# A two-layer hybrid-attention encoder on one core: where the grid heads' bias, values and outputs are issued, and when their probabilities are transposed

## The reference, cut to what matters

```python
sc = jnp.einsum('bnmiphd,bnmjqhd->bnmhipjq', qg, kg, ...) * (d ** -0.5)
sc = sc + bias.transpose(1, 2, 0, 3, 4, 5, 6)...[None]     # rpb: a learnt bias by row and column distance
sc = jnp.where(mask[:, :, None][None], sc, NEG_INF)
p = jax.nn.softmax(...)
o = jnp.einsum('bnmhipjq,bnmjqhd->bnmiphd', p.astype(v.dtype), vg)
```

## Time and profile before

| | us |
|---|---|
| median of 3 runs | 3005.68 (3001.18 to 3006.33) |
| the profiled execution | 3012.73 |
| its span | 3010.9 |
| TensorE busy | 2890.4 (96%) |
| VectorE, ScalarE, GpSimd busy | 1720.6, 1056.8, 26.3 |
| mean granted TensorE clock | 0.976 of full |

### The profile page before, as it was taken

The page is one execution under the profiler, slowest core; times in us unless marked ns, Lnnn a source line. Parts: engine busy times, 40 slices in busy tenths (PEclk is TensorE's granted clock), DMA queues, the critical chain, the costliest instruction groups (busy, mean ns, idle before and its releaser), DMA issues.

```text
span 3010.9 us, 39890 instructions
## 1 busy us (share of the span) xinstructions
PE 2890.4 (96%) x14640; PEld 2469.6 (82%) x14640; DVE 1720.6 (57%) x2998; ACT 1056.8 (35%) x1976; POOL 26.3 (1%) x53
## 2 busy tenths in 40 slices
PE   7999889998999999999999998999899999999998
PEld 7998777887888888888798987788788888888887
DVE  5642666885454554555666346678755555555457
ACT  5332655784311111111244245567742111111113
POOL 0000000000000000000000000000000000000000
PEclk9999989999999999999999998999999999999999
DMA  5656765323011111111146577553131111111111
GB/s 190 188 173 173 170 143 126 90 62 119 29 56 42 45 53 42 56 42 63 44 174 198 168 189 155 133 123 85 43 112 43 56 42 42 56 42 56 42 60 68
DMA packets 211031, 285.31 MB, mean 95 GB/s; under 512 B 64208, under 2 KB 170320, under 8 KB 201168
## 3 DMA queue, kind: packets, MB, share of 16 engines
q1 hardware_dynamic: 207056, 266.76, 31.5%
q0 software_dynamic: 3840, 16.78, 1.5%
HBM read 210.60 MB, written 72.88 MB: 94 GB/s over the span
## 4 chain that ended last, share of the span: by engine, by line
PE 81%; DVE 5%; DMA 5%; issue 3%; SPq 3%; ACT 2%; DVEq 1%; ACTq 0%; POOLq 0%
PE ps L1384 23%; PE ps L1213 20%; PE ps L1399 17%; PE ps L1286 7%; PE ps L1300 5%; PE ps L1329 4%; DMA head<-feats 3%; PE ps L1339 1%; PE ps L1181 1%; PE ps L1250 1%; DMA values<-vst 1%; SPq L463 1%; DVE x L1134 1%; SPq L488 1%; PE ps L1322 1%
## 5 line engine op out<-in xcount | busy, mean ns | idle before, releaser
L1399 PE MATMUL ps<-w_dn,hid 128*128 128x512 f32 x3072 | 712.9, 391 | 1.4
L1384 PE MATMUL ps<-hT,w_up 128*128 128x512 f32 x3072 | 702.5, 390 | 3.3 <-DVE hT L871 3.3
L1399 PEld LDWEIGHTS ps<-w_dn,hid 128*128 128x128 f32 x3072 | 573.8, 188 | 131.7 <-DVE x L1134 14.1
L1384 PEld LDWEIGHTS ps<-hT,w_up 128*128 128x128 f32 x3072 | 576.4, 188 | 122.9 <-ACT rbuf L821 3.7
L1213 PE MATMUL ps<-ws,hT 128*128 128x384 f32 (+3 forms) x3072 | 609.6, 357 | 2.6 <-issue 1.6
L1213 PEld LDWEIGHTS ps<-ws,hT 128*128 128x128 f32 x3072 | 538.1, 191 | 48.8 <-issue 2.4
L1134 DVE TENSOR_TENSOR x<-ps,x 128x512 f32<-128x512 f32 x512 | 342.8, 689 | 223.5 <-PE ps L1399 223.2
L772 ACT ACTIVATE pT<-ps 128x512 fp32r<-128x512 f32 (+1 forms) x448 | 240.2, 581 | 185.6 <-PE ps L1300 183.9
L1121 DVE TENSOR_TENSOR vbuf<-rbuf 128x512 f32<-128x512 f32 x128 | 88.6, 692 | 371.0 <-ACT rbuf L821 371.0
L871 DVE TENSOR_TENSOR pT<-ps,pT 128x512 fp32r<-128x512 f32 (+1 forms) x448 | 281.5, 664 | 8.6 <-ACT pT L772 6.7
L779 ACT ACTIVATE prob<-ps,a_nm 128x1024 f32<-128x1024 f32 (+1 forms) x256 | 252.6, 987 | 65.6 <-DVE a_nm L1036 49.7
(11 more groups left out here) (82 smaller groups left out, 2063.7 us busy)
## 6 DMA issues: line engine op xcount, KB each, us to landing
raw<-in_wstream SPq DMA_DIRECT2D x76, 1024.0 KB, 4.9
head<-feats SPq DMA_DIRECT2D x192, 256.0 KB, 6.4
feats<-tst SPq DMA_DIRECT2D x128, 192.0 KB, 2.6
values<-vst POOLq DMA_DIRECT2D x32, 384.0 KB, 3.2
head<-values SPq DMA_DIRECT2D x24, 512.0 KB, 4.2
biasC<-in_bias_c SPq DMA_DIRECT2D x16, 768.0 KB, 9.6
raw<-in_wstream SPq DMA_DIRECT2D x12, 768.0 KB, 5.9
x_park<-x SPq DMA_DIRECT2D x16, 512.0 KB, 9.4
```

The source lines that it names most:

```text
L1384: last = pe.matmul(ps[:, k % 2, :], w_up[0 if first else 1][:, w1, kt, ft * P:(ft + 1) * P], hT[:, w2, kt, sh * 512:(sh + 1) * 512], start ...
L1399: last = pe.matmul(ps[:, 2 + m % 4, :], hid[slot][:, w1, ft, s * P:(s + 1) * P], w_dn[1 if last_group else 0][:, w2, ft, nh * 512:(nh + 1) ...
```

## The change

A grid head's two bias halves are issued directly behind its features. Its sixteen value transfers, the eight transfers of a finished grid head's output and the one that reads it back are issued by GpSimd's queue instead of SP's, with the same waits and a semaphore of their own for the values. GpSimd waits for the end of the projections and of all their stores first. The transposes of a C item come three steps behind its scores instead of two; those of A and B stay at two. The weighing of a C block follows its transposes and so moves by one step as well. Where the kinds change from C to A, one step then has the transposes of two items.

```diff
--- before.py
+++ after.py
@@ -88,7 +88,7 @@
 NB = NI // 4
 GRID_BEFORE = [sum(kind_ == "C" for kind_, _, _ in ITEMS[:n_]) for n_ in range(NI)]
 STEPS = NI + 12
-TURN_STEP = [n_ + 2 for n_ in range(NI)]
+TURN_STEP = [n_ + (3 if kind_ == "C" else 2) for n_, (kind_, _, _) in enumerate(ITEMS)]
 WEIGH_STEP = [TURN_STEP[4 * b_ + 3] + 1 for b_ in range(NB)]
 
 
@@ -315,7 +315,7 @@
         tab_in, kr_in = sem("tab_in"), sem("kr_in")
         head_in = [sem(f"head_in{k}") for k in range(2)]
         value_in = [sem(f"value_in{k}") for k in range(2)]
-        grid_parked, grid_back = sem("grid_parked"), sem("grid_back")
+        grid_v_in, grid_parked, grid_back = sem("grid_v_in"), sem("grid_parked"), sem("grid_back")
         biasc_in = [sem(f"biasc_in{k}") for k in range(2)]
         s_done, mx_ready, p_ready = sem("s_done"), sem("mx_ready"), sem("p_ready")
         t_done, t_hi, t_lo = sem("t_done"), sem("t_hi"), sem("t_lo")
@@ -415,31 +415,11 @@
 
                 kind, h = HEADS[n]
                 load_features(l, n)
-                if n >= 3 and HEADS[n - 3][0] == "C":
-                    read_grid(l, HEADS[n - 3][1] - HA - HB)
                 if kind == "C":
                     load_bias(l, 2 * (h - HA - HB))
-                load_values(l, n)
-                if n >= 2 and HEADS[n - 2][0] == "C":
-                    park_grid(l, n - 2)
-                if kind == "C":
                     load_bias(l, 2 * (h - HA - HB) + 1)
-
-            def park_grid(l, n):
-
-                k = HEADS[n][1] - HA - HB
-                sp.wait_ge(o_ready, l * NB + 2 * n + 2)
-                rows = grid_out[k].rearrange("(f r c) d -> f r c d", f=2, c=GRID_W)
-                for t in range(8):
-                    cb, hf = t // 2, t % 2
-                    sp.dma_start(rows[hf, :, 16 * cb:16 * cb + 16, :], oC[k % 2][:, t, :]).then_inc(grid_parked, 16)
-
-            def read_grid(l, k):
-
-                h = HA + HB + k
-                sp.wait_ge(grid_parked, (l * HC + k + 1) * 8 * 16)
-                sp.dma_start(O[:, :, h * HD:(h + 1) * HD], grid_out[k].rearrange("(t p) d -> p t d", p=P))\
-                  .then_inc(grid_back, 16)
+                else:
+                    load_values(l, n)
 
             def load_bias(l, nc_half):
                 if nc_half >= 2:
@@ -475,18 +455,9 @@
                 hb = words(head[k][:, :])
                 if n >= 2:
                     sp.wait_ge(pv_done, l * NB + 2 * (n - 1))
-                if kind != "C":
-                    sp.dma_start(hb[:, 4096:5120].rearrange("p (t d) -> p t d", d=P),
-                                 values[:, h * P:(h + 1) * P].rearrange("(t p) d -> p t d", p=P))\
-                      .then_inc(value_in[k], 16)
-                else:
-                    grid = values.rearrange("(r c) d -> r c d", c=GRID_W)
-                    for cb in range(4):
-                        for rr in range(4):
-                            dst = hb[32 * rr:32 * rr + 32, 3072 + 512 * cb:3072 + 512 * (cb + 1)]
-                            src = grid[rr:rr + 13:4, c_cols(cb):c_cols(cb) + CKC, h * P:(h + 1) * P]
-                            sp.dma_start(dst.rearrange("c (g d) -> c g d", d=P),
-                                         src.rearrange("g c d -> c g d")).then_inc(value_in[k], 16)
+                sp.dma_start(hb[:, 4096:5120].rearrange("p (t d) -> p t d", d=P),
+                             values[:, h * P:(h + 1) * P].rearrange("(t p) d -> p t d", p=P))\
+                  .then_inc(value_in[k], 16)
 
             def stores_done(l):
 
@@ -602,6 +573,38 @@
         def _(pool):
 
             pool.memset(eps[:, :], EPS).then_inc(eps_set, 1)
+
+            def load_grid_values(l, n):
+
+                h, k = HEADS[n][1], n % 2
+                if n >= 2:
+                    pool.wait_ge(pv_done, l * NB + 2 * (n - 1))
+                grid = values.rearrange("(r c) d -> r c d", c=GRID_W)
+                for cb in range(4):
+                    for rr in range(4):
+                        dst = words(head[k][32 * rr:32 * rr + 32, 3072 + 512 * cb:3072 + 512 * (cb + 1)])
+                        src = grid[rr:rr + 13:4, c_cols(cb):c_cols(cb) + CKC, h * P:(h + 1) * P]
+                        pool.dma_start(dst.rearrange("c (g d) -> c g d", d=P),
+                                       src.rearrange("g c d -> c g d")).then_inc(grid_v_in, 16)
+
+            def park_grid(l, n):
+
+                k = HEADS[n][1] - HA - HB
+                pool.wait_ge(o_ready, l * NB + 2 * n + 2)
+                rows = grid_out[k].rearrange("(f r c) d -> f r c d", f=2, c=GRID_W)
+                for t in range(8):
+                    cb, hf = t // 2, t % 2
+                    pool.dma_start(rows[hf, :, 16 * cb:16 * cb + 16, :], oC[k % 2][:, t, :])\
+                        .then_inc(grid_parked, 16)
+
+            def read_grid(l, n):
+
+                h = HEADS[n][1]
+                k = h - HA - HB
+                pool.wait_ge(grid_parked, (l * HC + k + 1) * 8 * 16)
+                pool.dma_start(O[:, :, h * HD:(h + 1) * HD], grid_out[k].rearrange("(t p) d -> p t d", p=P))\
+                    .then_inc(grid_back, 16)
+
             for l in range(DEPTH):
                 for vt, e in enumerate(VSTAGED):
                     k = vt % 2
@@ -610,6 +613,23 @@
                     h0, nh = {"uv": (0, HA), "bv": (HA, HB), "cv": (HA + HB, HC)}[e[1]]
                     pool.dma_start(values[e[2] * P:(e[2] + 1) * P, h0 * P:(h0 + nh) * P],
                                    words(vst[:, k, 0:nh, :].rearrange("p h d -> p (h d)"))).then_inc(vst_out[k], 16)
+                pool.wait_ge(acc_done, l * len(ACCS) + job_end("cv"))
+                hold(pool)
+                for k in range(NTS):
+                    pool.wait_ge(tst_out[k], (l + 1) * 16 * TST_N[k])
+                    hold(pool)
+                for k in range(2):
+                    pool.wait_ge(vst_out[k], (l + 1) * 16 * (len(VSTAGED) // 2))
+                    hold(pool)
+                grids = [n for n in range(NH) if HEADS[n][0] == "C"]
+                for n in grids:
+                    load_grid_values(l, n)
+                    if n > grids[0]:
+                        park_grid(l, n - 2)
+                        read_grid(l, n - 2)
+                park_grid(l, grids[-1])
+                read_grid(l, grids[-1])
+
 
         @block.scalar
         def _(act):
@@ -1309,8 +1329,11 @@
                     if part == 0:
                         pe.wait_ge(t_lo, l * NGR + ITEM_GROUPS[4 * b + 3][-1] + 1)
                         n, k = b // 2, b // 2 % 2
-                        done = sum(VALUE_DMAS[kd] for kd, _ in HEADS[k:n + 1:2])
-                        pe.wait_ge(value_in[k], (l * VALUE_N[k] + done) * 16)
+                        if kind == "C":
+                            pe.wait_ge(grid_v_in, (l * HC + h - HA - HB + 1) * 16 * 16)
+                        else:
+                            done = sum(kd != "C" for kd, _ in HEADS[k:n + 1:2])
+                            pe.wait_ge(value_in[k], (l * VALUE_N[k] + done) * 16)
                         if b >= 2:
                             pe.wait_ge(o_ready, l * NB + b - 1)
                             pe.wait_ge(ot_ready, l * NB + b - 1)
@@ -1429,9 +1452,8 @@
 TST_N = [sum(stores_of(e) for e in STORED[k::NTS]) for k in range(NTS)]
 TST_BEFORE = [stores_before(n % NTS, n) for n in range(len(STORED))]
 HEAD_DMAS = {"A": 6 + 4, "B": 6, "C": 6}
-VALUE_DMAS = {"A": 1, "B": 1, "C": 16}
 HEAD_N = [sum(HEAD_DMAS[kd] for kd, _ in HEADS[k::2]) for k in range(2)]
-VALUE_N = [sum(VALUE_DMAS[kd] for kd, _ in HEADS[k::2]) for k in range(2)]
+VALUE_N = [sum(kd != "C" for kd, _ in HEADS[k::2]) for k in range(2)]
 def turn_of(stg):
 
     e = STAGED[stg]
```

## The result

| | before | after |
|---|---|---|
| median of 4 runs, us | 3005.79 (3001.18 to 3006.33) | 2978.36 (2977.35 to 2984.46) |
| profiled execution, its span | 3012.73, 3010.9 | 2977.77, 2975.8 |
| TensorE busy | 2890.4 (96%) | 2862.6 (96%) |
| GpSimd busy, instructions | 26.3, 53 | 141.7, 253 |
| mean granted TensorE clock | 0.976 | 0.989 |

The ratio is 0.9916, with a 95% interval of 0.9899 to 0.9934: 27.4 us faster, where 29 were forecast.

The account below looks back on a forecast made before the run. TensorE, busy 96% of the span, was taken as the bound, with its idle time and lowered clock. -64.5 + 25.2 + 10.2 = -29.1 us gave a median of 2977 us, own range 2965 to 2990, over the cases 2950 to 3004.

Parts of the forecast that it names:

- Parts 1 and 2 together: Grid heads C1 to C3, both layers: early bias and GpSimd's queue remove 33.1 us idle and 31.4 of slow clock.
- Part 1: Grid heads: both bias halves behind the features, next features following at once; both waits gone, -33.1 us idle, -31.4 slow clock.
- Part 2: Grid values and outputs on GpSimd's queue: frees SP of 7.47 + 4.96 us of issuing per grid head, cost 0.
- the window for the values: Between two grid weighings on TensorE: 17.5 us for sixteen GpSimd transfers needing 11.8, so 5.7 us to spare.
- Rival 2: First weighing of C1 to C3: GpSimd's issuing becomes the bound, values late, about 3045 us at 1.3 us each; chance 0.1.
- Part 3: C transposes one step later: removes no remaining wait, costs +25.2 us idle and +10.2 of lowered clock.
- idle at the change of kind: Where C gives way to A: TensorE idle 1.1 and 2.05 us, together 3.15, at eight changes, +25.2 us.
- lowered clock: After the short idle at C-to-A changes: TensorE's clock falls, costing 1.7 us at six changes, +10.2 us.
- The first grid head: C0's stretch, bias table to A1's features: order changes where TensorE waits, cost 0, within 2 us either way.

Follow-up runs that it names:

- e1: Changed kernel with grid-item transposes back at two steps behind their scores, early bias halves and GpSimd queue kept; 2938.52 us, ratio to before 0.9782.
- e3: Kernel before with the second bias half issued right behind the first, values and outputs still on SP's queue; 2983.07 us, ratio to before 0.9923.
- e7: e1 with only the parked outputs and their read back on GpSimd's queue, values on SP's; 2936.56 us, ratio to before 0.9772.
- e8: e1 with only the values on GpSimd's queue, outputs and read back on SP's; 2987.18 us, ratio to before 0.9936.
- e6: Changed kernel with a grid head's values in 32 transfers of half the size instead of 16; 2984.50 us, ratio to before 0.9935.
- e9: Changed kernel with only items 4 to 7 of a grid head transposed three steps behind, the others two; 2981.01 us, ratio to before 0.9920.
- e4: Changed kernel with only items 0 to 3 of a grid head transposed three steps behind, the others two; 2949.99 us, ratio to before 0.9818.
- e5: Changed kernel run again without an edit; 2978.16 us, ratio to before 0.9909.
- e2: Kernel before with the later transposes of grid items alone; 3060.06 us, ratio to before 1.0184.
- e10: e7 with the B heads' table loaded behind the fourth head's transfers instead of ahead of the second's; 2935.44 us, ratio to before 0.9768.
- e11: e7 run again without an edit, beside e10 on one chip; 2935.98 us, ratio to before 0.9773.

## Why the prediction was right, and where it was not

- **Parts 1 and 2 together, -64.5 us: right.** e1 has them alone and gains 67.1 us (3005.57 - 2938.52). The idle time was 37.5 us rather than 33.1: the third row of the two views, 4.4 us, belonged to the same stalls and went with them.
- **Which part earns it: wrong.** The step that failed is the end of Part 1, "I take both waits as gone", with Part 2's sentence that SP's issuing time was what "nothing but Part 1 needed". Part 1 has the features follow at once, and they do only where SP no longer waits for the finished output, which is Part 2. e3 is Part 1 alone and gains 22.5 us, since the features stay behind SP's wait for the finished output and come 6 us late. The other 44.5 us come with Part 2, and e7 and e8 show that they come with its eight output transfers and their wait, and not with the 7.47 us of issuing the values that the prediction put first. Moving the values gains nothing that can be told (e7 against e1: 2 us, inside the intervals).
- **Part 2, the window for the values: held.** I gave it 17.5 us; in C1 it was 354.49 to 374.27, 19.8 us. I gave the landing 3.2 us, from stores in the projections; it was 7.7 in the median. By these medians the room was 19.8 - 15 x 0.55 - 7.7 = 3.8 us, where I had 5.7; by the last transfer's own landing it was 1.6 to 3.0 us. The lock between VectorE and GpSimd that the Trainium skill describes (SBUF — State Buffer, "Who interferes with whom") did not show: the issues inside the heads took 552 ns in the median and 579 at most, while VectorE was busy for 77% of the time (6.65 of 8.69 us in C1). Its large operations there read PSUM and at most one tensor of SBUF, and outside the two-port modes that section says such instructions don't contend with GpSimd. (The 620 and 3100 ns that the prediction gives under that heading stand in another section of the same page of the Trainium skill, "A bandwidth-pool intuition that's wrong (but worth ruling out)", for a `tensor_copy` of VectorE.) e6 used the room up with 17 us of issuing and was late in half of its heads. Rival 2 had the right place and the right kind of price, and a break at 0.89 us per transfer lies between the measured 0.55 and e6's 1.06.
- **Part 3, idle at the change of kind, 3.15 us: right in mechanism.** Measured 0.94 + 1.89 = 2.83, eight times, 22.6 us against 25.2. e9 against e4 puts it on the last four items.
- **A term was missing.** The weighing of a block waits for the division of the block two before it. Its merge comes a step later with the transposes, and meets a step that has lost its own. 1.08 us, six times, 6.5 us. e4 keeps that step and moves the merge back, and the wait is gone; e9 keeps the later merge and fills the step, and 0.74 us of it stay. So the later merge makes the wait, and the missing transposes add 0.34 us.
- **Part 3, lowered clock, 1.7 us six times: mis-sized.** The six left out the two changes behind C0. Of the six, three had a slow stretch in the profiled execution, and of the two behind C0 one; in e5's execution it was six of all eight. Each cost 1.2 us: from A1 to A4 layer 1 with three of them took 134.49 us, layer 0 with none 130.75.
- **A second term was missing.** Without a slow stretch the changed kernel took 13.8 us more than e1 from A1 to A4 (130.75 against 116.91), and only 11.7 of it are waits. The other 2.1 us are in TensorE's busy time, 118.78 against 116.62 for the same matmuls, so 0.7 us per change of kind. Why they take longer isn't shown.
- **Part 3 adds up:** 22.6 + 6.5 of waits, 8 x 0.7 of longer work and 4 x 1.2 of lowered clock are 39.5 us; the medians of e1 and the changed kernel differ by 39.8.
- **The sum** was -29.1, from -64.5 and +35.4, and is -27.4, from -67.1 and +39.8. That it is so close is in part luck: two missing terms (6.5 and 5.6 us) stand against smaller idle times, rarer and cheaper slow stretches, and a wait left out of the gain.
- **The first grid head**: from the start of the heads to A1's first scores it took 43.22 us for 42.99 in layer 0, and 42.19 for 42.61 in layer 1: within 2 us, as bounded. Its wait moved from A1's features to C0's own, 2.14 us in layer 0 and 3.27 in layer 1, and in layer 0 to the bias behind them, 2.35.
- **e2's expectation failed** for a reason that the prediction had too: I priced the later transposes on the engines only. What waits for the weighing on a queue moves with it.

## What to carry to other kernels

A queue written out in program order hands each wait on to all transfers behind it, so what is to be moved off it is the transfer with the late wait, not the one that takes long to issue. In e7 the values' 7 us of issuing stayed on SP at no cost, while the wait for a finished output with its eight transfers cost 44 us (e3 against e1) to 49 (e8 against e1). The wait and the 5 us of issuing behind it were not tried apart. A change in several parts deserves a run of each part alone, since here one part gave back 40 of the 67 us that the others earned. Later is not safer in a software pipeline: a step more between scores and transposes holds banks and buffers that the next kind of work needs, and delays everything that waits for the end of the stage.

## What the runs showed of the hardware

- An issue on GpSimd's queue took 0.54 to 0.55 us for 384, 64 and 32 KB alike (the projections' values in the earlier trace rows, the changed kernel, e6). It took 0.60 us for the grid outputs, 32 KB in 128 pieces, and 0.93 for the read back, which has 1024 pieces of 256 bytes where the others have 64 or 128.
- Sixteen transfers of 64 KB from GpSimd's queue landed after 7.7 us in the median beside the next head's features (the changed kernel), and after 2.4 us without them (e8).
- Sixteen values on SP's queue took 7.5 us to issue in C1, at a DMA share of 0.43, but 10.3 and 15.8 us in C0 (e10 and e11), at a share of 1.06.
- The same idle times, 0.94 and 1.89 us within 4.3 us, lowered the granted clock to about 0.5 of full (1.2 instead of 2.4 GHz) for 3.4 us in some cases and not in others, in one execution as well as between two: four of eight, and six of eight.
